# Sample attention with queries and probabilities as the stationary operand, in four column groups

## The reference, cut to what matters

```python
ATTN_GROUPS = ((128, 1), (512, 4), (2048, 16))        # window, dilation; 4 heads of 64 each
def _dilated_attn_step(q, k_new, v_new, buf, dil, span, window):
    kk = jnp.concatenate([buf[:, :, 0], k_new], axis=1)
    vv = jnp.concatenate([buf[:, :, 1], v_new], axis=1)
    idx = Lb + jnp.arange(T)[:, None] - dil * jnp.arange(span + 1)[None, :]
    s = jnp.einsum("bthd,btkhd->bhtk", q, kk[:, idx]) * (Dh ** -0.5)
    p = jnp.exp(s - m)
    o = jnp.einsum("bhtk,btkhd->bthd", p, vv[:, idx]) / den
```

## Time and profile before

| what | us |
|---|---|
| median of 3 runs | 2257.8 |
| lowest and highest run | 2248.11, 2265.64 |
| span of the profiled execution | 2244.1 |
| this phase in the span | about 671 to 905 |

### The profile page before, as it was taken

The page is one execution under the profiler, slowest core; times in us unless marked ns, Lnnn a source line. Parts: engine busy times, 40 slices in busy tenths (PEclk is TensorE's granted clock), DMA queues, the critical chain, the costliest instruction groups (busy, mean ns, idle before and its releaser), DMA issues. The chain is left out here.

```text
span 2244.1 us, 29448 instructions
## 1 busy us (share of the span) xinstructions
PE 1954.9 (87%) x11877; PEld 1754.8 (78%) x11877; DVE 1203.5 (54%) x1221; ACT 817.8 (36%) x1163; POOL 390.4 (17%) x359
## 2 busy tenths in 40 slices
PE   7999999989977999888866697995799999999970
PEld 7899999978867999777753597974688888888850
DVE  5343334146543220255544444423888888888856
ACT  4211111124331220122231422222577777777732
POOL 0000000064424000211132000000552211111103
PEclk9999999989977899899978799996899999999985
DMA  6355554454426553533224733334799999999957
GB/s 221 124 162 162 162 162 162 148 170 134 125 67 182 157 148 104 181 101 111 101 82 137 269 121 93 136 122 163 297 405 405 411 407 403 408 405 405 403 221 254
DMA packets 202985, 472.97 MB, mean 211 GB/s; under 512 B 34391, under 2 KB 160759, under 8 KB 189794
## 3 DMA queue, kind: packets, MB, share of 16 engines
q1 hardware_dynamic: 134818, 319.29, 40.0%
q10 hardware_dynamic: 51440, 78.21, 9.6%
q0 software_dynamic: 16592, 73.60, 9.5%
HBM read 376.12 MB, written 121.93 MB: 222 GB/s over the span
## 5 line engine op out<-in xcount | busy, mean ns | idle before, releaser
L2642 DVE TENSOR_TENSOR k_w_lo<-expert_raw,k_w_hi 128x4096 fp32r<-128x4096 f32 x96 | 424.2, 4420 | 71.0 <-ACT k_w_hi L2586 71.0
L2586 ACT CAST k_w_hi<-expert_raw 128x4096 fp32r<-128x4096 f32 x96 | 348.3, 3631 | 107.7 <-PE k_pu L74 68.2
L72 PE MATMUL a_acc<-a_w_hi,x_hi 128*128 128x256 f32 x648 | 185.8, 287 | 0.0
L73 PE MATMUL a_acc<-a_w_lo,x_hi 128*128 128x256 f32 x648 | 183.8, 284 | 0.0
L74 PE MATMUL a_acc<-a_w_hi,x_lo 128*128 128x256 f32 x648 | 183.7, 283 | 0.0
L72 PEld LDWEIGHTS a_acc<-a_w_hi,x_hi 128*128 128x128 f32 x648 | 124.9, 193 | 0.1
L73 PEld LDWEIGHTS a_acc<-a_w_lo,x_hi 128*128 128x128 f32 x648 | 124.9, 193 | 0.0
L74 PEld LDWEIGHTS a_acc<-a_w_hi,x_lo 128*128 128x128 f32 x648 | 124.7, 193 | 0.0
L72 PE MATMUL k_pu<-k_w_hi,k_x_hi 128*128 128x512 f32 x256 | 104.9, 410 | 8.7 <-DVE k_w_lo L2642 8.7
L72 PE MATMUL k_po<-k_w_hi,k_h_hi 128*128 128x512 f32 x256 | 102.4, 400 | 10.6 <-DVE k_h_lo L2663 10.6
L948 PE MATMUL d_z_acc<-d_z_w_hi,x_hi 128*128 128x256 f32 x288 | 93.9, 326 | 16.5 <-DVE d_z_w_lo L934 14.8
(11 more groups left out here) (447 smaller groups left out, 5004.7 us busy)
## 6 DMA issues: line engine op xcount, KB each, us to landing
expert_raw<-in_w_expert_gate SPq DMA_DIRECT2D x32, 2048.0 KB, 9.9
expert_raw<-in_w_expert_up SPq DMA_DIRECT2D x32, 2048.0 KB, 11.5
expert_raw<-in_w_expert_down SPq DMA_DIRECT2D x32, 2048.0 KB, 11.2
scratch_o_moe<-k_out ACTq DMA_DIRECT2D x32, 512.0 KB, 11.4
a_w<-in_w_in SPq DMA_DIRECT2D x15, 1024.0 KB, 6.9
scratch_u_tm<-h ACTq DMA_DIRECT2D x81, 128.0 KB, 1.9
scratch_o_moe<-h_zeros POOLq DMA_DIRECT2D x2, 4096.0 KB, 29.0
out_s_kv<-in_cache_kv_w POOLq DMA_DIRECT2D x8, 1008.0 KB, 8.2
```

Of the source, the lines that this page charges most:

```text
L72: nc.tensor.matmul(out, one_pass(a_hi), one_pass(b_hi), start=(i == 0), stop=False)
L73: nc.tensor.matmul(out, one_pass(a_hi), one_pass(b_lo), start=False, stop=False)
L2586: nc.scalar.copy(one_pass(w_hi[:, kind, :]), raw[:, c % NRAW, :]).then_inc(s_hi, 1)
L2642: nc.vector.tensor_tensor(one_pass(w_lo[:, kind, :]), raw[:, c % NRAW, :], w_hi[:, kind, :], ALU.subtract).then_inc(s_lo, 1)
```

## The change

The roles of the operands are swapped. A cache unit is no longer a sequence but one chunk of 128 rows of four sequences (512 KB, two DMAs of 64 partitions); there are 18 key units and 18 value units, six buffers deep (`raw`). The 4 sequences x 4 heads x 8 tokens of a half are the 128 rows of the scores.

- **Scores** (`scores`, line 1345 after): for each of four sequences and two pairs of heads, the stationary operand is the sequence's 32 query columns, the moving operand 128 columns of transposed keys, and the output the 32 partitions that belong to the sequence: 8 matmuls for a unit, in column groups 0, 1, 2, 3, 0, 1, 2, 3. For the dilated groups POOL prepares queries with zeros for tokens that don't use the chunk (`chunk_queries`, 8 small copies for a half). New keys: 6 matmuls for each half (line 1354).
- **Softmax** works on rows as they come from PE, one half at a time, directly from PSUM. The first half's is placed in the middle of the keys, the second's behind them. The probabilities are turned once (6 transposes for a half, line 1363), and ACT copies them in 10 pieces into `PT`, zero outside of a chunk's tokens (`take_probs`).
- **Values** (line 1380): for each unit 4 matmuls, stationary 32 columns of probabilities, moving 256 columns of values, one in each column group; 3 matmuls for a half's new values (line 1372). ACT copies a finished half (line 1275), PE turns it with 2 transposes (line 1391), DVE makes 4 copies.
- Keys: 8 transposes for a unit, in two groups of 4, each followed by half a z unit; there is no drain; ACT copies 128x512 at a time (36 copies for the 48 of 128x384). On SP z block 1 is now asked for ahead of `stats`.

```diff
+        UNITS_K = 2 * CT
+        NR, NK = 6, 3
+        TURN_P = 11
+        JOIN_AT = (1, 3, 5, 7, 12, 13, 14, 15)
...
+                def scores(k):
+                    half, c = divmod(k, CT)
+                    g, c = place(c)
+                    pe.wait_ge(s_kte, turned_items(k))
+                    if g == 0 and half == 1:
+                        pe.wait_ge(s_read, 1)
+                    if g == 1 and c == 0:
+                        pe.wait_ge(s_chunk, half + 1)
...
+                    for hp in range(2):
+                        for j in range(HB):
+                            q = q_all[:, 0, hp, HB * half + j, :, :] if g == 0 else q_chunk[:, g - 1, c, hp, j, :, :]
+                            last = nc.tensor.matmul(p_row[32 * j:32 * j + 32, 0, g * 128:(g + 1) * 128],
+                                                    q.rearrange("p h t -> p (h t)"), kT[:, 2 * j + hp, :],
+                                                    start=(hp == 0 and c == 0), stop=(hp == 1 and c == last_chunk))
...
+                def values(v):
+                    n = UNITS_K + v
+                    half, c = divmod(v, CT)
+                    pe.wait_ge(s_raw[n % NR], 32 * (n // NR + 1))
+                    for j in range(HB):
+                        last = nc.tensor.matmul(p_row[32 * j:32 * j + 32, half, 0:GW], PT[:, c, 32 * j:32 * j + 32],
+                                                raw[:, n % NR, j, :], start=False, stop=(c == CT - 1), skip_group_check=True)
...
-                for b in range(NB):
-                    u = b % 2
-                    pe.wait_ge(s_k[u], (b // 2 + 1) * 64)
-                    for q in range(G):
...
-                        if q in (1, 2, 4):
-                            z.multiply(pe, 2 * (3 + 2 * b) + (1, 2, 4).index(q))
-                    pe.drain()
-                    pe.sem_inc(s_kfree, 1)
...
+                for k in range(UNITS_K):
+                    turn_keys(k, 0)
+                    z.multiply(pe, 2 * (3 + k))
+                    turn_keys(k, 1)
+                    z.multiply(pe, 2 * (3 + k) + 1)
+                    scores(k)
+                    if k % CT == CT - 1:
+                        scores_new(k // CT)
+                    if k == TURN_P:
+                        turn_probs(0, turned_items(k))
+                    if k in JOIN_AT:
+                        turn_joined(JOIN_AT.index(k))
+                for v in range(UNITS_K):
+                    if v == 0:
+                        unit(21)
+                        values_new(0)
+                    elif v == CT:
+                        turn_probs(1, turned_items(UNITS_K - 1))
+                        unit(21 + v)
+                        values_new(1)
+                        turn_outputs(0)
+                    elif 21 + v < Z_UNITS:
+                        unit(21 + v)
+                    values(v)
+                turn_outputs(1)
```

More of the change, by code:

```diff
@@ L1078, in _, with chunk_queries @@
                 pool.wait_ge(s_rot, 1)
+                nc.gpsimd.memset(work[:, 0:2048], 0.0)
+                pool.drain()
+                def chunk_queries(half):
+                    for g in (1, 2):
+                        for c in range(4):
+                            t = tokens_of(g, c)
+                            last = nc.gpsimd.tensor_copy(
+                                q_chunk[:, g - 1, c, :, :, :, t].rearrange("p x j h t -> p x (j h) t"),
+                                q_all[:, g, :, HB * half:HB * half + HB, :, t].rearrange("p x j h t -> p x (j h) t"))
+                            pool.drain()
+                    pool.sem_inc(s_chunk, 1)
@@ new lines, in _ @@
+                for t in range(4):
+                    join(t)
+                    if t >= 1:
+                        take_joined(t - 1)
+                take_joined(3)
+                z.split(dve, 2)
+                softmax(0)
+                for t in range(4, NP):
+                    join(t)
+                    if t > 4:
+                        take_joined(t - 1)
+                take_joined(NP - 1)
+                z.split(dve, 3)
+                softmax(1)
+                take_outputs(0)
@@ new lines, in scores @@
+                def scores(k):
+                    half, c = divmod(k, CT)
+                    g, c = place(c)
+                    pe.wait_ge(s_kte, turned_items(k))
[3 more added lines that the diff above has]
+                        pe.wait_ge(s_chunk, half + 1)
+                    last_chunk = 0 if g == 0 else 3
+                    for hp in range(2):
+                        for j in range(HB):
[3 more added lines that the diff above has]
+                                                    start=(hp == 0 and c == 0), stop=(hp == 1 and c == last_chunk))
+                    last.then_inc(s_scored, 1)
@@ new lines, in scores_new, with turn_probs @@
+                def scores_new(half):
+                    for g in range(3):
+                        for hp in range(2):
+                            q = q_all[:, g, hp, HB * half:HB * half + HB, :, :].rearrange("p j h t -> p (j h t)")
+                            last = nc.tensor.matmul(p_row[:, 1, g * 128:(g + 1) * 128], q, kTn[:, g, hp, :],
+                                                    start=(hp == 0), stop=(hp == 1))
+                    last.then_inc(s_sc, 1)
+                def turn_probs(half, n):
+                    pe.wait_ge(s_p, half + 1)
+                    for part in range(2):
+                        dst = item(n + part)
+                        for i in range(3):
+                            last = nc.tensor.transpose(dst[:, i, :], S[:, half, 3 * part + i, :], ident[:, :])
+                        last.then_inc(s_kt, 1)
@@ new lines, in values_new @@
+                def values_new(half):
+                    pe.wait_ge(s_pte, half + 1)
+                    if half == 0:
+                        pe.wait_ge(s_read, 2)
+                    for g in range(3):
+                        c0 = 2 * AW + g * GW
+                        nc.tensor.matmul(p_row[:, half, 0:GW], PT[:, CT + g, :], new[:, c0:c0 + GW], start=(g == 0), stop=False,
+                                         skip_group_check=True)
+                def values(v):
[5 more added lines that the diff above has]
+                                                raw[:, n % NR, j, :], start=False, stop=(c == CT - 1), skip_group_check=True)
+                    last.then_inc(s_pv, 1)
@@ L1246, in _, with turn_outputs @@
+                def turn_outputs(half):
+                    pe.wait_ge(s_ov, half + 1)
+                    if half:
+                        pe.wait_ge(s_done, 1)
+                    else:
+                        pe.wait_ge(s_taken, NP)
+                    for hp in range(2):
+                        last = nc.tensor.transpose(p_join[:, hp, :], S[:, half, hp, :], ident[:, :])
+                    last.then_inc(s_ovt, 1)
                 unit(0)
```

373 lines of the change are left out of this document (174 added, 199 removed).

## The result

The changed kernel takes **2186.1 us** (median of 4 runs, 2183.7 to 2187.4), against 2253.0 us for the kernel before (4 runs, 2242.9 to 2265.6): a ratio of 0.967, with a 95% interval of 0.963 to 0.970. The time of a run is its span and 1.9 us more: 2187.4 us for the profiled execution, whose span is 2185.5.

A forecast was written before the change was run, and what follows sets the result against it. PE's own instruction list was taken to bound the phase. The terms summed to -49.5 us against the span of 2244.1, giving 2194.6; with 13.7 us from span to median, 2208 us, range 2188 to 2236.

The forecast's parts named there:

- Scores and values: PE's score and value matmuls: column groups overlap, so scores fall from 33.4 to 15.8 us, values from 33.1 to 9.7.
- Switches of width: PE going between 128 and 32 columns: 72 switches at 0.04 us each, +3 us.
- Drains: PE's key loop: eight drains go, 0.3 us each, -2.4 us.
- Smaller things: PE's new keys, new values and output transposes added, the transposes of line 1296 removed: together +1.9 us.
- Start: PE's 4.99 us stall at the phase's start shrinks because z block 1 is asked for ahead of `stats`: -3 us.
- Hand-offs: Places losing cover, at the probabilities' ten ACT copies and the last values: +5 us, bounds +2 and +12.
- Clock: PE's clock loss of 26.8 us in the phase: two thirds of some 20 us regained, -13 us, bounds 0 and -20.
- the last line of the sum: Whole program: 13.7 us between profiled span and median, added to 2194.6 to give 2208 us.
- Program order: Rival, scores and values: column groups start in program order, 13.8 us more, 2222 us; chance 0.10.
- No overlap: Rival, scores and values: column groups don't overlap, 37.4 us more than forecast, 2246 us; chance 0.09.
- The DMA bound: Rival: the cache's DMAs become the phase's bound, landings holding the rate to 160 GB/s, 2233 us; chance 0.07.
- each record waits out: Rival, scores and values: each narrow record waits until the one before has left the array, 2315 us; chance 0.04.

The follow-up runs named there:

- e2: The changed kernel with the scores of all four sequences sent to column group 0 (results garbage); 2204.8 us, 0.976 of the kernel before.
- e8: The kernel before without the drain behind its key transposes, SP waiting for the transposes' own semaphore instead; 2257.2 us, ratio 0.998.
- e4: The changed kernel with both first key copies ahead of a z store on ACT and softmax weights ahead of the z split on DVE; 2176.2 us.
- e1: The kernel before with each score and value record moving 128 columns instead of 4 or 16 (results garbage); 2226.6 us, ratio 0.985.
- e5: The changed kernel with the scores' loops swapped, so the four records of one column group stand next to each other; 2188.0 us.
- e3: The changed kernel with the values of all four sequences sent to column group 0 (results garbage); 2209.3 us, 0.977 of the kernel before.
- e7: The changed kernel with 3 buffers of cache units instead of 6, same bytes; 2186.0 us, 0.968 of the kernel before.
- e10: The kernel before with only the scores moving 128 columns, values still narrow (results garbage); 2245.6 us, ratio 0.993.

## Why the prediction was right or wrong

**Scores and values: right, by the mechanism forecast.** Predicted were 15.8 us and, with switches, 17.3; measured 18 x 0.67 = 12.1. The 0.055 us a record came from two groups and was an upper value for four, which take one in 0.025 to 0.036. That the narrow records of before are paid for their stationary operand is argued and not shown: in e2 a record takes 0.111 us with an operand of 32 columns too, then with 128 moving ones. Values: predicted 9.7 and, with switches, 11.2; measured 14 x 0.76 and 2.0 for the last four blocks, 12.7. Four groups give (1.66 + 0.11)/(0.37 + 0.11) = 3.7 times the rate of one. Together 24.8 us for 28.5.

**Switches of width: too small, inside the terms above.** Entering and leaving costs 2 x (0.21 - 0.118), some 0.2 us for a scores block and 0.3 for a values block. With 18 and 15 stays that is 8 us and not 3. The working took 36 stays; there are 33. The Trainium skill's rule, TensorEngine Tiling (Array Packing), section Key Properties, that a change of tiling mode drains TensorE, is nearer to this (e8's drain took 0.34 us) than the one 27-column record on which I relied. Whether PE really drains there no run shows. The faster groups made it good, which was luck.

**Drains: right.** 0.34 us each in e8's timeline, for 0.3.

**Smaller things: right.** New keys +1.6, new values +1.4, outputs +0.8, line 1296's transposes -1.6: +2.2 us for +1.9.

**Start: wrong, and too small to show in the sum.** -3 us forecast, -0.6 measured. I followed the DMA that came earlier and not the queue behind it: on ACT the second copy stood behind a store with a table load, on DVE the weights behind the split. e4 shows both.

**Hand-offs: too dear, and not where they were expected.** +5 forecast; measured are one wait of 0.89 us in the key loop and 0.49 us at the end. PE waits nowhere behind the ten copies of probabilities (the first half's run on ACT from 759.33 to 760.7 us), for which +2 was reserved. The 0.89 us stand ahead of the scores of key unit 10, before the copies have begun:

```profile
753.75 0.64 PE L1345 MATMUL d_prow<-d_work 128*32 128x128 f32 x16 [0.89 <-ACT d_work L1244]
```

```profile
747.65 1.28 ACT L1249 ACT_TABLE_LOAD   x1
748.95 0.94 ACT L1249 ACTIVATE d_new<-d_new,d_mx 128x768 f32<-128x768 f32 x1
...
751.02 1.28 ACT L959 ACT_TABLE_LOAD   x1
...
753.11 0.58 ACT L1244 COPY d_work<-d_pkt 128x512 f32<-128x512 f32 x1 [0.40 <-ACT d_z_out L959]
```

The first half's Exp needs a table load, and the next store of a z unit another, ahead of the second key copy. That is the start's mechanism once more; the forecast had no term for it, and e4, which moves only the first store, still has this wait (0.9 us).

Without the clock these terms were to give -36.5 us, and they gave a little more. The phase shrank by 59.4 us, 20.0 of them clock by the two stretches (26.8 - 6.8), so 39.4 by work; the whole program's work went from 2075 to 2040 us, by 35.

**Clock: the step that failed, with the last line of the sum.** The mechanism was right and its size wrong, twice. For the profiled execution the term was -13 with bounds of 0 and -20; measured is -20, at the bound. Worse was the last line, the 13.7 us between span and median, which I added as if it were fixed. Only 1.9 us are (the time around a span). The rest was clock, by the split of the runs: the profiled execution lost 168 us, a run at the comparison's median of 2253.0 lost 2251.1 - 2075 = 176, the median of the 35 runs 183, the changed kernel 144. So against the median the clock gives back 32 to 39 us, not 13. The miss of 22 us is made up of 13 of that constant (13.7 for 0.6 us between span and median now), 7 of the clock term and 3 of the work, less the 0.7 that all else took more. The sentence "I take back two thirds" had its reason, narrow records ahead of each fall, and e1 shows that it was a reason for all of it: with 128 columns in each record, and 288 + 288 of them as before, both loops run at 1.00. So the width of the records is enough to keep the clock; whether shorter blocks of 4 and 16 columns would have kept it too, no run shows.

**The rivals.** Program order is excluded by e5 (and by 0.025 us a record). No overlap is what e2 and e3 build; both together, which wasn't run, would come to 2186 + 18.6 + 23.2 = 2228 us by this estimate, close to e1's 2226.6 and still faster than before, since the clock stays up in both. That separation is what the forecast lacked: of the 67 to 76 us between before and after, 35.5 are to be had from wider records alone (e1), and some 40 (2226.6 - 2186.1) come from column groups and the rest, about as much as e2 and e3 give back (41.8). The DMA bound is excluded by the waits (none for the cache), by e7, and by the rate: the phase moved 188 GB/s, where 160 was the rival's condition. That each record waits out would have shown 0.27 us between starts.

**What the forecast said would show it.** Four starts within 0.15 us: they lie within 0.02. Clock of 0.95 or more: it is 0.96. Stall under 2.5 us at the start: no, it is 4.4. No wait for the cache: there is none.

## What to carry to other kernels

Read the granted clock of the loop that a change touches in more than one execution, and split each run into span x clock and span x (1 - clock): a difference between the profiled execution and the median is a term of the sum, and may be just what the change removes. Matmuls that move few columns cost twice: here 0.109 us a record whether it moved 4 or 128 columns, and the clock of the wide work around them; more moving columns per record gave about half of this gain without one record fewer. When a transfer comes earlier, follow each in-order queue behind it down to the copy that the bound engine waits for, table loads included.

## What the runs showed of the hardware

- PE's clock falls to 1.2 GHz while PE is never idle, behind records of 4 or 16 moving columns that lie 0.109 us apart (e10: 0.66 over 55 us of full business). The same records with 128 columns keep it at 1.00 (e1).
- How far it falls differs by execution: 1.00 and 0.92 over the same 44.4 us in two profiles of before, 0.65 in e8's with the same value loop. The spread of before (25 us over 35 runs) goes with the clock's loss (166 to 192 us, correlation 0.91) and not with the work (0.00).
- Four column groups start within 0.02 us (0.04 in e5) and keep separate orders: 16 records of 128 columns take 0.64 and 0.66 us in the two orders, 1.93 us in one group.
- The Trainium skill, TensorE: Matmul & The Clock Gate, Part 3, section The mechanism, has matmuls start and end strictly in order. e5's 0.66 us disagree for records in different column groups; within one group, where they start 0.109 us apart, no run here speaks against it.
- A stay in the narrow mode (operands of 32 columns) costs 0.2 us beyond its records with 128 columns, 0.3 us with 256; 1.2 GHz also came around the one long stall of 4.4 us, from 702 to 708.7 us.
